# Wide pieces of the feed-forward blocks: 512- and 256-column products grouped by size instead of alternating

## What is computed

```python
def sq_relu_mlp(h, w1, w2):                      # M0, M1: 1024 -> 4096 -> 1024
    z = jax.nn.relu(jnp.einsum('bsd,df->bsf', h, w1))
    return jnp.einsum('bsf,fd->bsd', z * z, w2)

def swiglu(x, w_gate, w_up, w_down):             # F1, F2: 1024 -> 2816 -> 1024
    return (jax.nn.silu(x @ w_gate) * (x @ w_up)) @ w_down
```

## Time and profile before

| | |
|---|---|
| median of three runs | 1010.08 us (1009.28 to 1010.40) |
| profiled execution, its span | 1008.6 us |
| PE busy | 1001.3 us, 99% |
| PE weight loads busy | 857.4 us, 85% |
| DVE busy | 683.2 us, 68% |
| ACT busy | 556.0 us, 55% |
| instructions | 14152 |

### The profile page before, as it was taken

One profiled execution on the slowest core, in us unless ns is written; L12 is line 12 of the kernel. 1 busy time (PEld: TensorE's weight loads), 2 busy tenths in 40 slices (PEclk: granted clock), 3 DMA queues, 4 the chain that ended last, 5 costly groups with the idle time before them and its releaser, 6 DMA issues.

```text
span 1008.6 us, 14152 instructions
## 1 busy us (share of the span) xinstructions
PE 1001.3 (99%) x5620; PEld 857.4 (85%) x5620; DVE 683.2 (68%) x925; ACT 556.0 (55%) x804; POOL 34.5 (3%) x37
## 2 busy tenths in 40 slices
PE   9999999999999999999999999999999999999997
PEld 7988788888889988888888888888888788888886
DVE  5777676666667887666566767565668867666564
ACT  6678654444446866444444655545467664645453
POOL 1000010000002300000000100000010010000000
PEclk9999999999999999999999999999999999999999
DMA  9943385665563545755655566665625465665621
GB/s 334 307 157 126 126 273 176 201 210 173 172 204 112 181 167 188 243 175 172 207 206 167 176 216 195 211 201 178 200 87 147 136 199 170 224 209 167 209 84 43
DMA packets 124559, 184.80 MB, mean 183 GB/s; under 512 B 3162, under 2 KB 103182, under 8 KB 124366
## 3 DMA queue, kind: packets, MB, share of 16 engines
q1 hardware_dynamic: 122304, 176.70, 53.3%
q0 software_dynamic: 1728, 6.60, 1.8%
q10 hardware_dynamic: 462, 0.60, 0.2%
HBM read 182.81 MB, written 1.07 MB: 182 GB/s over the span
## 4 chain that ended last, share of the span: by engine, by line
PE 96%; DVE 3%; ACT 1%; issue 0%; POOL 0%; DVEq 0%; POOLq 0%
PE bank L1532 36%; PE bank L1509 28%; PE bank L1511 14%; PE bank L1495 3%; PE bank L1497 3%; PE bank L1498 3%; PE bank L1707 1%; PE bank L1558 1%; DVE w_lo L829 1%; PE bank L1683 1%; PE bank L1653 1%; PE bank L1667 1%; DVE work L1006 0%; PE bank L1852 0%; PE bank L1853 0%; PE bank L1854 0%
## 5 line engine op out<-in xcount | busy, mean ns | idle before, releaser
L829 DVE TENSOR_TENSOR w_lo<-raw,w_hi 128x2048 fp32r<-128x2048 f32 x164 | 374.0, 2290 | 130.6 <-ACT w_hi L426 130.5
L1509 PE MATMUL bank<-xT,w_hi 128*128 128x512 f32 x1216 | 431.3, 398 | 0.0
L1511 PE MATMUL bank<-xT,w_lo 128*128 128x256 f32 x1216 | 341.0, 280 | 0.0
L426 ACT ACTIVATE w_hi<-raw 128x2048 fp32r<-128x2048 f32 x164 | 311.7, 1908 | 35.6 <-PE bank L1532 32.7
L1509 PEld LDWEIGHTS bank<-xT,w_hi 128*128 128x128 f32 x1216 | 228.4, 188 | 55.7 <-issue 0.3
L1511 PEld LDWEIGHTS bank<-xT,w_lo 128*128 128x128 f32 x1216 | 229.5, 189 | 1.9
L1532 PE MATMUL bank<-w_hi,z_hi 128*128 128x512 f32 x472 | 153.5, 393 | 0.1
L1532 PE MATMUL bank<-w_lo,z_hi 128*128 128x512 f32 x472 | 152.3, 391 | 0.0
L1532 PE MATMUL bank<-w_hi,z_lo 128*128 128x512 f32 x472 | 151.7, 390 | 0.0
L470 ACT ACTIVATE work<-bank 128x256 f32<-128x256 f32 x152 | 49.8, 380 | 178.5 <-PE bank L1511 178.5
L904 DVE TENSOR_TENSOR work<-bank,work 128x256 f32<-128x256 f32 x152 | 57.1, 418 | 73.9 <-ACT work L470 73.9
(11 more groups left out here) (213 smaller groups left out, 771.4 us busy)
## 6 DMA issues: line engine op xcount, KB each, us to landing
raw<-in_w SPq DMA_DIRECT2D x64, 1024.0 KB, 5.3
raw<-in_f_gate SPq DMA_DIRECT2D x22, 1024.0 KB, 5.4
raw<-in_f_up SPq DMA_DIRECT2D x22, 1024.0 KB, 5.9
raw<-in_f_down SPq DMA_DIRECT2D x22, 1024.0 KB, 5.0
raw<-in_w_in SPq DMA_DIRECT2D x11, 1024.0 KB, 5.5
raw<-in_w_qkv SPq DMA_DIRECT2D x9, 1024.0 KB, 9.0
raw<-in_w_o SPq DMA_DIRECT2D x4, 1024.0 KB, 5.0
raw<-in_rec_w_o SPq DMA_DIRECT2D x4, 1024.0 KB, 5.8
```

The costliest lines, as they stand in the source:

```text
L426: e.activation(*by_channel(n, w_hi[n % RING], raw[n % RAW]), ACT.Copy).then_inc(hi_done, 1)
L829: e.tensor_tensor(low_, here, high, ALU.subtract).then_inc(lo_done, 1)
L1509: e.matmul(bank[i], whi[:, k, cut], xT[:, k, :, :].rearrange("p b s -> p (b s)"), start=(k == 0), stop=False, skip_group_check=True)
L1511: last = e.matmul(bank[i][:, 0:S], wlo[:, k, cut], xT_hi[:, k, :], start=False, stop=(k == KB - 1), skip_group_check=True)
```

## The change

The wide pieces get functions of their own. `wide_high` makes the two 512-column products of one k, `wide_low` the two 256-column ones. `wide_piece` waits for `w_hi` alone, makes all 16 long products, waits for `w_lo`, and makes all 16 short ones; a step between (`spread`) now hangs on the k of the short ones, in F2 on k = 0 instead of 4. `first_wide_piece` does it in two halves of four k each, with the transposes behind k = 1 of the long products as before. `u_piece` and `first_u_piece` lose their parameter and serve `u_block` alone. The same products with the same operands are made; within a bank the sums are added up in another order.

```diff
+        def wide_high(n, k, banks):
             whi = w_hi[n % RING].rearrange("p (k c) -> p k c", k=KB)
+            for b, i in enumerate(banks):
+                e.matmul(bank[i], whi[:, k, b * P:(b + 1) * P], xT[:, k, :, :].rearrange("p b s -> p (b s)"),
+                         start=(k == 0), stop=False, skip_group_check=True)
+
+        def wide_low(n, k, banks):
             wlo = w_lo[n % RING].rearrange("p (k c) -> p k c", k=KB)
             for b, i in enumerate(banks):
-                cut = slice(b * P, (b + 1) * P)
-                e.matmul(bank[i], whi[:, k, cut], xT[:, k, :, :].rearrange("p b s -> p (b s)"), start=(k == 0),
-                         stop=False, skip_group_check=True)
-                last = e.matmul(bank[i][:, 0:S], wlo[:, k, cut], xT_hi[:, k, :], start=False, stop=(k == KB - 1),
-                                skip_group_check=True)
+                last = e.matmul(bank[i][:, 0:S], wlo[:, k, b * P:(b + 1) * P], xT_hi[:, k, :], start=False,
+                                stop=(k == KB - 1), skip_group_check=True)
             return last
+        def wide_piece(n, banks, inside=None):
+            e.wait_ge(hi_done, n + 1)
+            for k in range(KB):
+                wide_high(n, k, banks)
+            e.wait_ge(lo_done, n + 1)
+            for k in range(KB):
+                mm = wide_low(n, k, banks)
+                if k == KB - 1:
+                    mm.then_inc(used, 1)
+                if inside and k in inside:
+                    inside[k]()
+
+        def first_wide_piece(j, n, banks):
+            split(n)
+            for g in range(2):
+                for k in range(4 * g, 4 * g + 4):
+                    e.wait_ge(xlo_done, KB * j + k + 1)
+                    wide_high(n, k, banks)
+                    if k == 1:
+                        for i in range(4, KB):
+                            turn(j, i)
+                for k in range(4 * g, 4 * g + 4):
+                    mm = wide_low(n, k, banks)
+            mm.then_inc(used, 1)
...
-                    u_piece(f.ups(p) + i, f.banks(p, i), between if i == 0 else None, u_wide)
+                    wide_piece(f.ups(p) + i, f.banks(p, i), between if i == 0 else None)
...
-            first_u_piece(f.j, f.n0, f.banks(0, 0), u_wide)
+            first_wide_piece(f.j, f.n0, f.banks(0, 0))
             for i in range(1, f.nu):
-                u_piece(f.n0 + i, f.banks(0, i), None, u_wide)
+                wide_piece(f.n0 + i, f.banks(0, i))
             for p in range(1, f.pairs - 1):
-                ups(p, {7 if f.j == F1 else 4: lambda: spread(f.j)} if p == 1 and f.nu == 2 else None)
+                ups(p, {7 if f.j == F1 else 0: lambda: spread(f.j)} if p == 1 and f.nu == 2 else None)
```

More of the change, by code:

```diff
@@ L1500, in u_block, with u_piece @@
             return last
-        def u_wide(n, k, banks):
+        def wide_high(n, k, banks):
             whi = w_hi[n % RING].rearrange("p (k c) -> p k c", k=KB)
+            for b, i in enumerate(banks):
+                e.matmul(bank[i], whi[:, k, b * P:(b + 1) * P], xT[:, k, :, :].rearrange("p b s -> p (b s)"),
+                         start=(k == 0), stop=False, skip_group_check=True)
+        def wide_low(n, k, banks):
             wlo = w_lo[n % RING].rearrange("p (k c) -> p k c", k=KB)
             for b, i in enumerate(banks):
-                cut = slice(b * P, (b + 1) * P)
-                e.matmul(bank[i], whi[:, k, cut], xT[:, k, :, :].rearrange("p b s -> p (b s)"), start=(k == 0),
-                         stop=False, skip_group_check=True)
-                last = e.matmul(bank[i][:, 0:S], wlo[:, k, cut], xT_hi[:, k, :], start=False, stop=(k == KB - 1),
-                                skip_group_check=True)
-            return last
-        def u_piece(n, dst, between=None, block=u_block):
+                last = e.matmul(bank[i][:, 0:S], wlo[:, k, b * P:(b + 1) * P], xT_hi[:, k, :], start=False,
+                                stop=(k == KB - 1), skip_group_check=True)
+            return last
+        def wide_piece(n, banks, inside=None):
[21 more added lines that the diff above has]
+            mm.then_inc(used, 1)
+        def u_piece(n, dst, between=None):
             split(n)
             for k in range(KB):
-                mm = block(n, k, dst)
+                mm = u_block(n, k, dst)
                 if k == KB - 1:
@@ L1584, in closing_tokens, with first_u_piece @@
             d_part(n2, lhs2, 1, (0, 1), (1,), last=True).then_inc(used, 1)
-        def first_u_piece(j, n, dst, block=u_block):
+        def first_u_piece(j, n, dst):
             split(n)
```

## The result

The change makes the kernel faster: 1003.65 us (median of five runs, 1002.97 to 1004.56) against 1009.87 us for the kernel before (now five runs too, where the table above has three). The ratio is 0.994, 95% interval 0.9929 to 0.9951; 6.2 us are gone where 4.8 were forecast. One execution of the kernel before (1999.34 us) and one of experiment 3 (5642.45 us) lie far outside all others and are in no ratio.

What follows compares the result with a forecast made beforehand. PE, busy 99% of the span, bounds the kernel through the pace between products' starts. 5.4 + 0.3 - 0.9 = 4.8 us off 1010.1 gives 1005.3 us; the forecast's own range is 1003.2 to 1006.5, the overall range 1003.0 to 1008.1.

Steps and rivals of the forecast that it cites:

- Grouping by size: In 67 slow wide pieces, 16 long then 16 short products take 5.56 us instead of 5.64: 5.4 us gained.
- Down pieces behind two wide pieces: 20 down pieces, 5.50 us in F1 against 5.46 in M1, perhaps slowed by alternation ahead: 0.3 us gained.
- The first pieces: First piece of each block: fewer products ahead of the transposes, more behind them; together 0.9 us lost.
- The later wait: In wide pieces, the low weights are waited for half a piece later: worth nothing.
- the spread products: In F2 they move 0.35 us later, with 2.6 us of slack before the down piece: nothing.
- Rival 1: Order doesn't matter, the slow pace belongs to the stretch; only the first pieces' loss remains: 1011.0 us, chance 0.10.
- Rival 2: In wide pieces, a long product streaming xT costs 0.236 us by itself, a piece 5.70 us: 1015.0 us, chance 0.04.

Runs made afterwards that it cites:

- experiment 3: The change in all full wide pieces, but the first piece of each block alternates long and short products as before: 1003.0 us.
- experiment 6: The change with first pieces alternating as before, and in F1 and F2 the second of two wide pieces mirrored, 16 short products first: 1002.36 us.
- Experiment 8: The change with both waits, for w_hi and w_lo, at the start of each wide piece again: 1003.57 us.
- experiment 7: The change with first pieces in groups: long and short products of k = 0 and 1, transposes, k = 2 and 3, k = 4 to 7: 1002.96 us.
- experiment 5: The kernel before, with one more transpose ahead of each full wide piece of pair 1 and later: 1014.49 us (one run).
- experiment 1: The change with full wide pieces in groups of one k, two long products then two short ones, eight times: 1004.58 us.
- experiment 2: The change with full wide pieces in two groups of four k, eight long then eight short products, twice: 1005.12 us.

## Why the prediction was right, point by point

**Grouping by size**, the main term: right in mechanism, too small. The 67 pieces are 6.5 us shorter together, not 5.4. Of them 46 gain 0.10 us each instead of 0.08; the 18 that stand behind another grouped wide piece gain 0.08 (5.65 to 5.57), since their first long products follow short ones. The step that was mis-sized is "a down piece is 24 of them in 5.46 us ... 0.2275 us each": these 24 follow short products, and so hold the cost of a step themselves. Behind long ones they take 5.44 (experiment 6), 0.2267 each, and a piece's 16 then 3.63 instead of 3.64; with the first short product cheap as well (1.91 for 16 instead of 1.92), a piece is 5.54 instead of 5.56. The value was within the bounds given, near their upper end. Three pieces stand apart. M0's second gained 0.21 and M1's 0.16, with a wait and a gap that shrank. F1's fourth wasn't slow before (its last 14 pairs stood in 4.85 us) and lost 0.03.

**Down pieces behind two wide pieces:** 5.50 became 5.47, 0.03 each, 0.6 us for twenty, where 0.3 of a possible 0.8 was taken. M0's first down piece, no longer behind a wait, adds 0.08.

**The first pieces:** 0.9 us of loss forecast, 0.9 measured, and the mechanism as written: transposes that can't end earlier, with the short products moved behind them. M0's first piece is 0.43 us longer (0.42 forecast), F2's first four 0.54 (0.48), F1's first three 0.10 (0.1). M1's first is 0.15 shorter, for the reason given: the transposes go earlier; with the gap before its second piece gone as well, its gain is twice the 0.1 forecast, and its first down piece comes 12.02 us behind the block's start instead of 12.33. Experiment 8 shows that the gap is gone without the later wait. The prediction missed one wait, which the list of waits doesn't show: before, M0's first down piece stood some 0.13 us for `z_lo` (experiment 3). So the way to that down piece grew by 0.21 us only, and moving work ahead of the transposes (experiments 3 and 7) can give back no more than that there; over all four blocks it gives back 0.7 us.

**The later wait, and the spread products:** nothing, as said. F2's first z_lo is ready at 831.83 + 0.69 = 832.52 and its down piece starts at 835.20:

```profile
831.83 0.69 DVE L932 TENSOR_TENSOR z_lo<-work,z_hi 128x512 fp32r<-128x512 f32 x1 [0.70 <-ACT z_hi L485]
```

Together 6.5 + 0.7 - 0.9 = 6.3 us, and 6.23 before rounding, which is the blocks' sum. All terms came with the sign forecast; the time lies near the lower end of the forecast's own range because the main term was 1.1 us short.

**Rival 1** (the slow pace belongs to the stretch) fell, with a grain of truth in it: experiment 5 shows that one order does have two paces. At the fast pace the old order is as cheap as the new one: F1's second and third piece took 5.55 us and now take 5.57 and 5.56. So what grouping took away is the slow pace, and no grouped piece in these traces has shown a second pace.

The order-free gaps of the Trainium skill's "TensorE: Matmul & The Clock Gate", section "Back-to-back issue gap", fell with it. Its formula gives 216 ns for 512 columns and, as an estimate worked out from it, 109 ns for 256. The two products hold 227 and 120 ns here, and a step from one size to the other moves single products by 1 to 9 ns. The same section calls that formula the one for an isolated product and gives some 131 ns per 512-column product for a stream with weight loads; no product here comes near that.

**Rival 2** (a long product on xT costs 0.236 us) fell by the rows of the change: 16 of them in 3.63 us.

**A rival that was not priced:** the banks. Before, both products of a pair write one bank one after the other; grouped products take turns between two. No run changes the one without the other. Against it stands that neither size cares in a long run: long products keep 0.227 us in a down piece, where the banks take turns, and in the 36 at the end of M0, where six at a time go to one bank (8.20 us in the change); short ones keep 0.120 with one bank and with two (1.91 us for 16).

## What to carry to other kernels

When one engine is full, price its instructions by the distance between starts in a run of their own kind, and look at what stood ahead of that run: its first members may pay for the change of kind. Where long and short products can be put in any order, groups of one size kept clear of the slow pace here, and groups of two already get most of it; fewer changes of size are not always better, since seven steps before two long products each (experiment 1) cost a piece no more than one step before eight (experiment 2). Before moving work past an instruction that waits for another engine, ask whether that work was the cover: here the short products moved behind the transposes gave back 0.9 us of the gain, and a few moved ahead again recovered 0.7.

## What the runs showed of the hardware

All of this is at the full clock (1.00 in the stretches shown above). The first long products behind short ones are slow in a fixed pattern, 27 ns over the first five and nothing afterwards (5.47 against 5.44 us for 24). In the change the distances from start to start are 0.233, 0.236, 0.228, 0.233 and 0.231 us, then 0.227, the same for a down piece and for a wide one. In the timeline of the change, M1, the first pair of a down piece takes 0.47 us and the next two 0.46:

```profile
411.71 0.63 PE L1563 MATMUL bank<-w_hi,z_hi 128*128 128x512 f32 x2
412.18 0.62 PE L1563 MATMUL bank<-w_lo,z_hi 128*128 128x512 f32 x2
412.64 0.62 PE L1563 MATMUL bank<-w_hi,z_lo 128*128 128x512 f32 x2
413.10 0.61 PE L1563 MATMUL bank<-w_hi,z_hi 128*128 128x512 f32 x2
```

The first short one behind long ones is 7 ns cheaper than the 120 ns of the rest. The prices of the two sizes, 226.7 and 120 ns, differ by 107 ns for 256 columns; at that rate per column some 13 ns of each product, long or short, don't depend on its columns (an estimate from these two).

Strict alternation of 512 and 256 columns runs at one of two paces, 0.3465 or 0.353 to 0.354 us per pair, keeps it through a piece, and passes from one to the other at a piece's start. In experiment 5 it is 39 pieces to 30; in the kernel before, six full pieces near the start of F1 and F2 (F2's third is cut by the spread products) are fast and 66 are slow. Which buffer or queue makes this was not tried, and nothing here shows it.
